# Projecting the convolved columns channel-major and running their convolution beside the next tile, with the row mapping of the sample selection moved behind the first prompt rows

## What is computed

```python
(m_qk, m_v, m_o, m_gate, m_if, a_q, a_k, a_v, a_gate,
 i_q, i_w, i_k, c_q, c_gate) = split_in(rms_norm(x, g_pre) @ w_in)
qk, conv_state = causal_conv(m_qk, hist, conv_w, conv_b)   # 4 taps, 2048 channels, then silu
q = heads(qk[..., :MLSTM_W]); k = heads(qk[..., MLSTM_W:]) * MLSTM_DH ** -0.5   # 4 heads x 256
I = indexer_scores(iq, iw, ik, causal)     # sparse attention: 16 index heads x 64
_, idx = lax.top_k(I, top_k)               # 128 keys of 512 (prompt), 256 of 2052 (sample)
y = x + rms_norm(concat(m_out * silu(m_gate), a_out * silu(a_gate), c_out * silu(c_gate)) @ w_out)
```

## Time and profile before

| | |
|---|---|
| median of three runs | 1880.14 us (1877.06 to 1888.46) |
| profiled execution | 1877.01 us, its span 1875.3 us |
| mean granted TensorE clock | 0.937 |
| PE busy | 1679.8 us (90%) |
| DVE busy | 814.8 us (43%) |
| POOL busy | 673.4 us (36%) |
| ACT busy | 569.1 us (30%) |
| bytes moved | 249.01 MB, mean 133 GB/s |

### The profile page before, as it was taken

One profiled execution on the slowest core, in us unless ns is written; L12 is line 12 of the kernel. 1 busy time (PEld: TensorE's weight loads), 2 busy tenths in 40 slices (PEclk: granted clock), 3 DMA queues, 4 the chain that ended last, 5 costly groups with the idle time before them and its releaser, 6 DMA issues.

```text
span 1875.3 us, 20980 instructions
## 1 busy us (share of the span) xinstructions
PE 1679.8 (90%) x7801; PEld 1272.0 (68%) x7801; DVE 814.8 (43%) x1319; ACT 569.1 (30%) x876; POOL 673.4 (36%) x448
## 2 busy tenths in 40 slices
PE   6899999999999499998899999987658789799995
PEld 5677775677897376776688778865334455477774
DVE  6400010599929856755632161112465454501113
ACT  5522233222221233233222422224244443312221
POOL 3655531333333166766444444421110111033331
PEclk9999999999999699999999999998667788789997
DMA  6544431233344267766455544437404323542222
GB/s 214 160 134 130 142 101 56 71 105 108 92 120 144 77 196 231 221 197 211 122 154 165 149 134 117 147 125 230 93 29 152 107 68 107 192 160 85 83 78 106
DMA packets 139674, 249.01 MB, mean 133 GB/s; under 512 B 26504, under 2 KB 63308, under 8 KB 136296
## 3 DMA queue, kind: packets, MB, share of 16 engines
q10 hardware_dynamic: 66928, 122.86, 21.0%
q1 hardware_dynamic: 55920, 72.76, 12.2%
q0 software_dynamic: 16736, 52.18, 9.6%
HBM read 204.11 MB, written 43.66 MB: 132 GB/s over the span
## 4 chain that ended last, share of the span: by engine, by line
PE 73%; DVE 13%; DMA 5%; ACT 4%; issue 2%; POOL 1%; ACTq 1%; SPq 0%; DVEq 0%; POOLq 0%
PE acc L431 16%; PE acc L433 16%; PE acc L432 16%; PE acc L426 4%; PE acc L427 4%; PE ps_c L991 3%; PE acc L1722 2%; DVE arena L1669 1%; PE ps_c L2116 1%; PE acc L2111 1%; DMA arena<-z_prompt 1%; PE ps_a L1155 1%; POOL w_lo L389 1%; ACT z_tile L471 1%; PE ps_a L1224 1%
## 5 line engine op out<-in xcount | busy, mean ns | idle before, releaser
L389 POOL TENSOR_TENSOR w_lo<-w_raw,w_hi 128x1024 fp32r<-128x1024 f32 (+1 forms) x200 | 466.7, 2334 | 814.8 <-ACT w_hi L385 814.5
L431 PE MATMUL acc<-w_hi,x_hi 128*128 128x512 f32 (+1 forms) x1472 | 580.4, 394 | 8.8 <-DVE keep L925 5.3
L433 PE MATMUL acc<-w_hi,x_lo 128*128 128x512 f32 (+1 forms) x1472 | 565.9, 384 | 0.0
L432 PE MATMUL acc<-w_lo,x_hi 128*128 128x512 f32 (+1 forms) x1472 | 565.3, 384 | 0.0
L385 ACT CAST w_hi<-w_raw 128x1024 fp32r<-128x1024 f32 (+1 forms) x200 | 204.2, 1021 | 758.3 <-PE acc L427 716.6
L431 PEld LDWEIGHTS acc<-w_hi,x_hi 128*128 128x128 f32 x1472 | 278.8, 189 | 93.9 <-issue 28.0
L433 PEld LDWEIGHTS acc<-w_hi,x_lo 128*128 128x128 f32 x1472 | 278.1, 189 | 55.8
L432 PEld LDWEIGHTS acc<-w_lo,x_hi 128*128 128x128 f32 x1472 | 278.8, 189 | 51.4 <-issue 0.7
L426 PE MATMUL acc<-w_hi,x_hi 128*64 128x512 f32 (+1 forms) x368 | 141.4, 385 | 0.0
L427 PE MATMUL acc<-w_lo,x_hi 128*64 128x512 f32 (+1 forms) x368 | 140.9, 384 | 0.0
L2231 DVE TENSOR_TENSOR arena<-arena (+1 forms) x16 | 14.0, 887 | 176.8 <-ACT arena L464 176.8
(11 more groups left out here) (439 smaller groups left out, 1903.0 us busy)
## 6 DMA issues: line engine op xcount, KB each, us to landing
w_raw<-in_w_in ACTq DMA_DIRECT2D x136, 512.0 KB, 3.7
z_prompt<-z_tile ACTq DMA_DIRECT2D x68, 256.0 KB, 2.5
w_raw<-in_w_out ACTq DMA_DIRECT2D x32, 512.0 KB, 3.6
arena<-z_prompt SPq DMA_DIRECT2D x4, 2088.0 KB, 10.2
w_raw<-in_w_mem_kv ACTq DMA_DIRECT2D x16, 512.0 KB, 4.1
arena<-q_sample POOLq DMA_DIRECT2D x32, 256.0 KB, 4.0
arena<-z_prompt SPq DMA_DIRECT2D x10, 512.0 KB, 7.3
between<-z_prompt SPq DMA_DIRECT2D x10, 512.0 KB, 10.1
```

The source lines that it names most:

```text
L389: nc.gpsimd.tensor_tensor(out=w_lo[:, c % 2, :, 0:w], in0=w_raw[:, c % RAWS, :, 0:w], in1=w_hi[:, c % 2, :, 0:w].bitcast(F32), op=ALU.subt ...
L431: nc.tensor.matmul(acc[m][:, 0:w], xh, wh, start=first, stop=False)
L432: nc.tensor.matmul(acc[m][:, 0:w], xh, wl, start=False, stop=False)
L433: last = nc.tensor.matmul(acc[m][:, 0:w], xl, wh, start=False, stop=end)
```

## The change

**Tiles.** The four tiles of `m_qk` get the kind "t": weight columns stand still and the 512 rows stream, so that `acc[m]` holds 128 channels x 512 rows. The number of matmuls is the same. Their prompt part is copied out of PSUM unscaled and not stored. **Convolution.** In the first four calls of the following tile DVE multiplies one 128-channel piece by `rstd_bc` (each row's `rstd`, on all partitions), keeps the last three rows, and convolves it, all in SBUF; in call 5 of that tile ACT applies silu to the four pieces and issues their stores to a new DRAM tensor `qk_p`, channel-major. `rstd_bc` and the taps are made by `tensor_late_consts` and `vector_late_consts` ahead of the index tiles. **mLSTM stage.** `tensor_conv_turn`, `vector_conv` and `scalar_conv` of each head are gone, and q and k are loaded from `qk_p` straight into `qk_t`; the taps' loads move into `sync_tables`; the turning of the taps (a piece of `tensor_mlstm_gates`) and their copy on ACT are gone; `p_conv` is written by six transfers of SP out of SBUF instead of one inside DRAM. **Selection.** All 32 top-k rounds run ahead of the sample rows' preparation; `vector_physical` stays in call 7 (now `PREP_FIRST`), but PE turns its result in call 10 and DVE copies it in call 10 (`PHYS_PAUSE`), row r is scored in call 12 + r, and POOL's gather r is issued in call 13 + r. The diff, cut to its core (the removed functions stand above in the kernel before):

```diff
+                            if kind == "t":
+                                xh, xl = hi_t[:, k, 0:S], lo_t[:, k, :]
+                                wh, wl = (v[:, c % 2, i, m * P:(m + 1) * P] for v in (w_hi, w_lo))
+                                nc.tensor.matmul(acc[m][:, :], wh, xh, start=first, stop=False)
+                                nc.tensor.matmul(acc[m][:, :], wl, xh, start=False, stop=False)
+                                last = nc.tensor.matmul(acc[m][:, :], wh, xl, start=False, stop=end)
+                                continue
...
+                if kind == "t" and m < MT:
+                    nc.scalar.copy(z_tile[:, m, :], acc[m][:, :]).then_inc(acc_read, 1)
+                    continue
...
+                if c == CH - 2 and late is not None:
+                    late()
...
+            for dst, src in ((conv_nat[0:CK, :], I["conv_w"][0]), (conv_nat[CK:CK + 1, :], I["conv_b"][0:1, :])):
+                sp.dma_start(dst, src).then_inc(tables_in, 16)
...
+        def tensor_late_consts(pe):
+            pe.wait_ge(*at("rstd_spread"))
+            pe.wait_ge(tables_in, 16 * N_TABLES)
+            for m in range(MT):
+                nc.tensor.matmul(ps_c[:, m * P:(m + 1) * P], conv_a[:, m * P:(m + 1) * P], ident[:, :], start=True, stop=True)
+            for k in range(KT):
+                last = nc.tensor.transpose(ps_b[:, k * (CK + 1):(k + 1) * (CK + 1)], conv_nat[:, k * P:(k + 1) * P],
+                                           ident[0:CK + 1, 0:CK + 1])
+            last.then_inc(reached("late_turned"), 1)
+        def vector_late_consts(dve):
+            dve.wait_ge(rstd_ready, 2)
+            for m in range(MT):
+                last = nc.vector.tensor_copy(conv_a[:, m * P:(m + 1) * P], rstd(NU_MEM + m, P).broadcast_to([P, P]))
+            last.then_inc(reached("rstd_spread"), 1)
+            dve.wait_ge(*at("late_turned"))
+            nc.vector.tensor_copy(rstd_bc, ps_c[:, :])
+            nc.vector.tensor_copy(conv_c, ps_b[:, 0:KT * (CK + 1)].rearrange("p (k j) -> p k j", j=CK + 1)
+                                  ).then_inc(reached("late_copied"), 1)
+            dve.wait_ge(*at("late_copied"))
+        def vector_conv(dve, i, m):
+            k = 4 * i + m
+            dve.wait_ge(acc_read, acc_base(N_B0 + i) + m + 1)
+            dlink(nc.vector.tensor_tensor(out=conv_a, in0=z_tile[:, m, :], in1=rstd_bc, op=ALU.mult))
+            nc.vector.tensor_copy(last_rows(k // 8)[:, k % 8, :], conv_a[:, S - CK + 1:S])
+            out = z_tile[:, m, :]
+            dlink(nc.vector.tensor_scalar(out, conv_a, conv_c[:, k, CK - 1:CK], None, ALU.mult))
+            for j in range(1, CK):
+                ins = nc.vector.scalar_tensor_tensor(out=out[:, j:S], in0=conv_a[:, 0:S - j],
+                                                     scalar=conv_c[:, k, CK - 1 - j:CK - j], in1=out[:, j:S],
+                                                     op0=ALU.mult, op1=ALU.add)
+                if j < CK - 1:
+                    dlink(ins)
+            ins.then_inc(cv_tapped, 1)
+            dve.wait_ge(cv_tapped, k + 1)
+        def scalar_conv(act, i):
+            for m in range(MT):
+                k = 4 * i + m
+                act.wait_ge(cv_tapped, k + 1)
+                nc.scalar.activation(z_tile[:, m, :], z_tile[:, m, :], ACT.Silu, bias=conv_c[:, k, CK:CK + 1]).then_inc(cv_silu, 1)
+            for m in range(MT):
+                k = 4 * i + m
+                act.wait_ge(cv_silu, k + 1)
+                act.dma_start(qk_p[k * P:(k + 1) * P, :], z_tile[:, m, :]).then_inc(z_stored[m], 16)
...
-            sp.dma_start(O["p_conv"].rearrange("l b j c -> (l b j) c"), z_p[S - CK + 1:S, 0:2 * MW]).then_inc(conv_out, 16)
+            sp.wait_ge(cv_tapped, 4 * NCT)
+            for half in range(2):
+                for j in range(CK - 1):
+                    sp.dma_start(O["p_conv"][0, 0, j, half * MW:(half + 1) * MW].rearrange("(k p) -> p k", p=P),
+                                 last_rows(half)[:, :, j], allow_slow_non_contiguous=True).then_inc(conv_out, 16)
...
-            for i, c in enumerate((C_QK, C_QK + MW, C_O, C_G, C_V)):
+            for i in range(2):
+                src = qk_p[i * MW + h * MD:i * MW + (h + 1) * MD, :].rearrange("(d p) t -> p d t", p=P)
+                sp.dma_start(qk_t[h % 2][:, i, :, :], src).then_inc(zh_in[h % 2], 16)
+            for i, c in enumerate((C_V, C_O, C_G)):
                 src = z_p[:, c + h * MD:c + (h + 1) * MD].rearrange("(m p) c -> p m c", p=P)
-                dst = va[h % 2][:, :, 0:MD] if i == 4 else z_h[h % 2][:, i, :, :]
+                dst = va[h % 2][:, :, 0:MD] if i == 0 else z_h[h % 2][:, i - 1, :, :]
...
-            pe.wait_ge(conv_silu, 4 * (h + 1))
+            pe.wait_ge(zh_in[h % 2], zh_count(h))
...
-                    tensor_conv_turn(pe, h + 1, i)
...
-        TK0 = 25
         TKR = KSEL_S // 8
-        CK0 = TKR - TK0 + 3
+        PREP_FIRST = 7
+        PHYS_PAUSE = 10
+        CK0 = PHYS_PAUSE + 3
...
-            yield from hosted_pause(TKR - TK0 + 1)
+            yield from hosted_pause(PHYS_PAUSE)
             yield from tensor_physical(pe)
 
         def vector_rows(dve):
-            for i in range(TK0, TKR):
-                vector_topk_sample(dve, i, i + 1)
-                yield
-            yield from vector_physical(dve)
+            mapped = vector_physical(dve)
+            yield from hosted_pause(PREP_FIRST)
+            next(mapped)
+            yield from hosted_pause(PHYS_PAUSE - PREP_FIRST)
+            yield from mapped
...
-                scalar_tile(act, n, "b", steps)
+                i = n - N_B0
+                scalar_tile(act, n, "t" if i < NCT else "b", steps,
+                            late=(lambda i=i: scalar_conv(act, i - 1)) if 0 < i <= NCT else None)
...
+            vector_late_consts(dve)
             vector_index_prep(dve)
             vector_scores(dve)
-            vector_topk_sample(dve, 0, TK0)
+            vector_topk_sample(dve, 0, TKR)
             vector_sample_prep(dve)
             prompt, rows = vector_prompt(dve), chain(vector_rows(dve), hosted_pause(1), vector_gather(dve))
-            for _ in range(CH * NBT):
+            for i in range(CH * NBT):
                 next(prompt, None)
                 next(rows, None)
                 next(prompt, None)
+                if 0 < i // CH <= NCT and i % CH < MT:
+                    vector_conv(dve, i // CH - 1, i % CH)
...
-                tensor_tile(pe, n, "b", steps)
+                tensor_tile(pe, n, "t" if n - N_B0 < NCT else "b", steps)
             run(steps[0])
             run(steps[1])
             tensor_gather_out(pe)
-            beside_memory(tensor_mem_s(pe), tensor_mlstm_gates(pe), (4, 6, 9))
-            for u in range(4):
-                tensor_conv_turn(pe, 0, u)
```

More of the change, by code:

```diff
@@ L58, in hybrid_decoder_step @@
     NBT = C_IF // TN
+    NCT = 2 * MW // TN
     N_Y0 = N_B0 + NBT
@@ L85, in hybrid_decoder_step @@
         iw_s = scratch("iw_sample", [R, IH])
+        qk_p = scratch("qk_prompt", [2 * MW, S])
         ident = sb("ident", [P, P])
@@ L491, in tile_loop, with scalar_tile @@
                 body(n0 + 1)
-        def scalar_tile(act, n, kind, steps=NO_STEPS, often=False):
+        def scalar_tile(act, n, kind, steps=NO_STEPS, often=False, late=None):
             for c in range(1, CH + 1):
@@ L566, in hybrid_decoder_step @@
         gate_s = keep[:, 912:1040]
+        CK = 4
+        conv_nat = place(X_OFF, [2 * MW], CK + 1)
+        conv_a = place(X_OFF + 3112, [S])
+        conv_c = conv_cols[:, :].rearrange("p (k j) -> p k j", j=CK + 1)
+        last_rows = lambda half: small[:, 32 * half:32 * half + 24].rearrange("p (k j) -> p k j", j=CK - 1)
         POOL_PAGES = 2 * CH * IXT
@@ L1454, in hybrid_decoder_step @@
         GW = S + R
-        CK = 4
         row = lambda i: place(GW * i, [GW], H)
@@ L1462, in hybrid_decoder_step @@
         c_e = keep_m[:, 40:60].rearrange("p (m h) -> p m h", h=H)
[L1463 to L1475, removed]
+        mx_T = keep_m[0:H, 60:70]
+        bias_g = keep_m[0:H, 70:72]
+        m0_s = keep_m[0:H, 72:80]
+        a_T = keep_m[0:H, 80:88]
+        bn_o = keep_m[:, 88:96]
+        st_m = keep_m[:, 96:104]
+        aT8 = keep_m[0:NB, 104:108]
+        w_b = keep_m[0:R, 108:140].rearrange("p (h b) -> p h b", h=H)
+        batch_of = keep_m[0:R, 140:148]
+        head_rows = sb("head_rows", [P, H * P])
+        hr = head_rows[0:H, :]
+        rstd_bc = head_rows[:, :]
+        z_h = [place(M0, [2, MT, MD]), part(xl_free, 0, [2, MT, MD])]
         va = [place(M0 + 5120, [MT, MD + 2]), part(xl_free, 4096, [MT, MD + 2])]
         qk_t = [place(M0 + 7180, [2, 2, S]), part(xl_free, 5128, [2, 2, S])]
-        cv = [place(M0 + 6152, [S]), place(M0 + 6668, [S])]
         k_n = place(M0 + 9228, [MT, MD])
@@ L1494, in hybrid_decoder_step @@
         m0_nat = place(M0 + 12396, [H], NB)
-        (mc_in, xc_turned, xc_done, kn_turned, kn_done) = (
```

(17 more changed lines are left out.)

79 lines of the change are left out of this document (17 added, 62 removed).

## The result

The changed kernel took 1894.66 us (median of 5, 1890.51 to 1896.66), the one before 1877.71 beside it: a ratio of 1.0071, 95% interval 1.0052 to 1.0090. It is slower by 0.5 to 0.9%, where 1837 had been forecast. The profiled execution has a span of 1894.6 us against 1875.3.

The account below looks back on a forecast made before the run. PE was taken as the bound, its waits as the gaps to close. From 1877.0 us, gains of 88.6 and losses of 45 gave 1833.4, against the median 1836.5; forecast 1837, range 1800 to 1868 (likeliest case 1815 to 1862).

Parts of the forecast that it names:

- Gains A and B: b tiles: PE's waits for rotated block 0 (L1116) and the mapping (L832) close, with half-clock spells; 16.7 and 14.8 us.
- Rival 4: b tiles: the mapping's move does nothing, PE waits for block 0's attend instead; second gain falls to 2, 1850 us; chance 0.04.
- Gathers: b tiles: gathers issued one call closer to their reader hold DVE 2.8 us, 1.2 reaching PE in 12 calls; loss 14 us.
- three-quarters rule: Calls 12 to 41: ACT, DVE and gather losses, 53.6 us raw, overlap, so three quarters, 40, were counted.
- rival 3: Calls 12 to 41: PE waits for DVE, which waits for that call's gather; up to 84 us lost, 1910; chance 0.07.
- likeliest case: Whole kernel: the summed gains and losses hold, forecast 1837 us, range 1815 to 1862; chance 0.58.
- softmax's 3.5: b tiles: the sample's softmax, also asked for one call closer, costs 3.5 us.
- Convolution on DVE and ACT: b tiles: moved pieces lose 26 us on DVE, mostly in crowded calls, and 13.6 on ACT by silus and stores.
- Gain D: Ahead of head 0: four convolution pieces go, but the sample rows' preparation limits the gain to 18 us, not 30.
- Gain C: mLSTM gates: sixteen small transposes of the taps and an ACT copy leave the chain; 2.3 us gained.
- Gain E: Heads 1 and 2: without the next head's convolution they become like head 3 (35.6 us); 36.8 us gained together.
- Rival 2: Heads 1 and 2 stay long, by loads and updates wanting 215 GB/s or DVE's own chains; 1855 or 1873; chance 0.18.

Follow-up runs that it names:

- after: The changed kernel as made, with the whole change, against the kernel before: 1894.66 us, ratio 1.0071.
- e6: Kernel before with only the selection's part of the change, and POOL's gathers one call earlier than the change has them: 1848.05 us, ratio 0.9827.
- e4: Kernel before with only the selection's part of the change, gathers at call 13 + r as in the change: 1884.79 us, ratio 1.0024.
- e2: Changed kernel with POOL's gathers one call earlier, as far ahead of their reader as before: 1853.19 us, ratio 0.9863.
- e5: Changed kernel with gathers one call earlier and p_conv turned by PE, stored as 512-byte rows behind the loads of heads 0 and 1: 1828.66 us.
- e1: Changed kernel without the six transfers that write p_conv (that output left out): 1863.95 us, ratio 0.9911.
- e7: e5 with the three tap operations of each of the 16 moved convolution pieces left out (output wrong in value): 1810.66 us, ratio 0.9627.
- e8: e5 with the third tile's pieces convolved in calls 24, 27, 28 and 29, its silus in call 31: 1818.84 us, ratio 0.9666.

## Why the prediction was wrong, point by point
**Gains A and B** (31.5): right. The shift from call 6 to 9 is -31.6 in after and -28.3 in e6. That e6 as a whole kernel gives 32.5 (1877.7 x 0.0173) is partly luck, as it holds 8.6 of the third gap, which had no term. Rival 4 had nothing to it.

**Gathers**: the step that failed most. I took 14 before the three-quarters rule, and it was 41 (37 in e4 against e6). The sizing went by one call in which a gather issued at 734.75 would land 2.8 us too late, gave PE 1.2 of it in 12 calls, and called the rest slack. The runs showed fewer and longer waits: DVE waits for K rows in 15 of the 32 rounds, 66.4 us in all and up to 13.17 in one, and PE loses time at a few places behind them. After less e2, that is 9 us in call 17, 6 in calls 18 to 21, 5 in call 29, 8 in calls 30 to 36 and 13 in calls 43 to 47. The first place shows how. The gather is issued behind `w_lo` and lands 8.9 us later, so DVE scores only at 683.07 and begins block 1's rotations behind that (685.47; in e2 679.16), and PE waits for these in call 17. Then `w_lo` waits for `w_hi`, which waits for PE, and the next gather that DVE needs goes out late as well:

```profile
674.22 0.95 POOL L954 DMA_INDIRECT arena<-in_cache_attn_k,keep  x1 [0.31 <-issue]
683.07 1.23 DVE L979 TENSOR_TENSOR arena<-arena 128x1024 f32<-128x1024 f32 x1 [13.17 <-DMA arena<-in_cache_attn_k,keep]
695.73 1.09 PE L1189 MATMUL ps_a<-ident,arena 128*128 128x128 f32 x4 [8.03 <-DVE arena L1162]
708.29 2.40 POOL L391 TENSOR_TENSOR w_lo<-w_raw,w_hi 128x1024 fp32r<-128x1024 f32 x1 [12.10 <-ACT w_hi L387]
712.82 0.95 POOL L954 DMA_INDIRECT arena<-in_cache_attn_k,keep  x1 [0.30 <-issue]
717.50 2.04 DVE L979 TENSOR_TENSOR arena<-arena 128x1024 f32<-128x1024 f32 x1 [4.12 <-DMA arena<-in_cache_attn_k,keep]
```

In e2 PE waits 1.65 us at this L1189 and POOL 3.16 us at this L391. So the waits go round a ring, POOL to DVE to PE to ACT to POOL. They do not grow without end: DVE waits 3.46 us for the gather at 842.45, 6.82 at 853.64, and nothing at 860.62. My rival 3 had this order of waits, but in each of 30 calls, at up to 84 us and with a chance of 0.07; the likeliest case held it at 10. What I called the softmax's 3.5 (calls 45 to 47) is in the same loss: e2 shows none of it, and there the softmax's wait even shrinks, from 5.25 us to 2.21.

**p_conv**: the step that was missing. The one transfer of before took SP 0.79 us, and I costed its six successors at nothing, without a row for a store of single elements. Measured: 24.5 (e2 to e5) to 30.7 (after to e1), nearly all of it in the memory attention's stretch.

**Convolution on DVE and ACT**: right in kind and near in size. I gave 39.6 raw, times three quarters 30. At call 78 e5 stands at -4.2 and e6 at -34.6: 30.4, of which 3.7 lie ahead of call 6 (the late constants and what is around them, forecast 1.3) and 26.7 in the b tiles. The steps at ACT's blocks are 3.4 (forecast 3.4) in call 13, 0.6 in call 21, at most 3.1 in call 29 (e7) and 0.9 in call 37: 8 in all, where three quarters of my 13.6 is 10. Without the taps (e7) some 18 go, where three quarters of DVE's 26 is 19.5. The place was right: call 29, behind the crowded calls 24 to 27, for 18. A piece took longer than the 3.6 I gave: the group rows of after have its five operations at 0.82, 0.48 and three taps of 0.88 to 1.01.

```profile
L706 DVE SCALAR_TENSOR_TENSOR z_tile<-arena,conv_cols,z_tile 128x509 f32<-128x509 f32 x16 | 16.2, 1014 | 0.6
L706 DVE SCALAR_TENSOR_TENSOR z_tile<-arena,conv_cols,z_tile 128x511 f32<-128x511 f32 x16 | 14.4, 902 | 0.6
L706 DVE SCALAR_TENSOR_TENSOR z_tile<-arena,conv_cols,z_tile 128x510 f32<-128x510 f32 x16 | 14.0, 876 | 0.6
```

Against 0.75 with the operand in PSUM that is 0.18 more a tap on average, 9 us over 48. It is not spread over all of them. In after's timeline the 42 taps that meet no `w_lo` take 0.75 us each. Six meet one: two, which began 0.30 and 0.54 us ahead of it, take 0.75, the other four 2.76, 2.77, 2.98 and 3.17 us, which is the whole 9. One of these four, and its `w_lo`:

```profile
788.12 2.98 DVE L706 SCALAR_TENSOR_TENSOR z_tile<-arena,conv_cols,z_tile 128x509 f32<-128x509 f32 x1
788.15 2.40 POOL L391 TENSOR_TENSOR w_lo<-w_raw,w_hi 128x1024 fp32r<-128x1024 f32 x1
```

The Trainium skill's rule on the shared port ("SBUF — State Buffer", section "SBUF: two separate sides"), that one of the two operations holds the port for its whole length, agrees with these rows in kind. By its words the one that starts first goes first; by the profile's starts two of the four long taps began 0.03 and 0.26 us ahead of their `w_lo`. So the prediction's doubt about 3.6 us a piece was right in kind, and its 32 us, from one whole `w_lo` for each piece, too high: 4 of 48 taps met one so.

**Gain D** (18): 15.5. From SP's store of the mixed memory rows to L1746, the sums of head 0, it is 1441.93 - 1392.08 = 49.9 us, against 65.4 before (1325.50 to 1390.89). As said, the sample rows' chain and not PE sets it: PE waits 17.8 us for L1985. Gain C (2.3) was not measured by itself.

**Gain E** (36.8): 17.3 + 11.8 = 29.1. Windows of after, heads 1, 2 and 3:

```profile
1456.17:1493.50 37.33, 32.29 (x130) 16.89 (x130) 20.22 (x48) 13.71 (x29) 0.00 (x0) 0.90 0.64 204
1507.56:1549.20 41.64, 36.60 (x126) 18.43 (x126) 19.83 (x45) 13.72 (x29) 0.00 (x0) 0.78 0.59 183
1564.40:1600.00 35.60, 30.56 (x126) 15.86 (x126) 19.82 (x45) 13.60 (x29) 0.00 (x0) 0.94 0.45 140
```

Against the earlier trace rows head 1 fell from 54.60 to 37.33 and head 2 from 53.40 to 41.64. Rival 2 (the 215 GB/s) did not hold: 204 was reached, and 214 in head 2 of e2, at 35.7 us. Head 2 misses head 3 by 6 us at the same DVE work and count of matmuls; what differs is PE's granted clock, 0.78 against 0.94. It is no chance of one run: in each of the eleven kernels with the moved convolution one of heads 1 and 2 takes 41.6 to 42.2 us and the other 35.6 to 37.3. The term had no price for it, and with that the bound of 36.8 was about 8 too high.

**The sum with these numbers**: 1877.7 - 31.5 (A, B) - 47.7 (C, D, E, as e5 shows them from call 78 to the first y chunk: -4.2 to -51.9) + 30 (convolution, late constants) + 41 (gathers) + 27 (p_conv) = 1896.5, against 1894.7. The terms are differences between these same kernels, so this shows that they add up and nothing more.

## What to carry to other kernels
Where pieces of several engines are placed by call numbers, moving one means checking every pair of issuer and reader by its distance in calls: where the issuer hangs on the bound engine's progress, a wait of the reader comes back round to the issuer, and here PE lost about 40 us by DVE's 66 instead of having them hidden in DVE's idle time. A transfer that moves little data can still fill the DMA engines; before an output is stored in a new layout, count its runs, and turn it on PE if they are single elements. When a summed forecast meets crowded and empty calls, place each moved piece by the call's own load: here one shift of where the same work stands was worth 10 us (e8); that the second adds to it is not settled.

## What was not expected of the hardware
While 24 KB were stored as 6144 single elements, the DMA engines showed a busy share of 1.05 over 41 us at only 90 GB/s, and loads of another queue landed in 20.8 us instead of 6.6. And PE stayed at its half clock level (1.2 GHz of 2.4) while it was busy throughout. In head 2 of after it had the full level from 1500 to 1507.5, then worked 5.58 of the next 7.5 us, and then had half the clock for 12 us without an idle moment; head 3, with the same 126 matmuls, took 6 us less:

```profile
1500.00:1507.50 7.50, 7.11 (x40) 5.11 (x39) 5.05 (x21) 1.03 (x3) 0.97 (x1) 1.00 0.00 0
1507.50:1515.00 7.50, 5.58 (x14) 2.58 (x14) 4.32 (x5) 4.17 (x9) 0.00 (x0) 0.68 0.42 115
1515.00:1522.00 7.00, 7.00 (x17) 2.77 (x16) 1.94 (x4) 0.08 (x1) 0.00 (x0) 0.50 1.06 361
1522.00:1527.00 5.00, 5.00 (x13) 2.76 (x14) 1.57 (x3) 1.30 (x4) 0.00 (x0) 0.50 0.59 180
```

Four products of L2129 still take 2.07 us some 14 us into the head, and 1.13 behind that:

```profile
1521.82 2.07 PE L2129 MATMUL acc<-between,w_raw 32*128 32x256 f32 x4
...
1528.34 1.13 PE L2129 MATMUL acc<-between,w_raw 32*128 32x256 f32 x4
```

The stretch of 12 us also has full DMA engines (share 1.06 in its first part), but that alone is not the reason: head 1 of e5 has a share of 1.02 and the full clock in the same part of the head (1395 to 1402). What sets the moment at which the clock returns was not tried.
